# Attention inside a two-model transformer program: one more step of lag between scores and output, four calls joined into one, and a bias added on VectorE

## The reference

```
for one head and one block of 128 queries:
    s = q @ k.T * 64**-0.5  (+ bias, + mask)          # 128 x nk scores
    p = softmax(s)  (with a sink logit in two of them) # rows over nk keys
    o = p @ v
diff_attention:  pd = softmax(s0) - lam * softmax(s1);  o = pd @ v      # two maps, one output
```

## Time and profile before

| | |
|---|---|
| median of three runs | 4613.79 us (4609.85 to 4614.44) |
| the profiled execution | 4609.33 us |
| its span | 4607.6 us |
| TensorE matmul busy | 92% of the span |
| VectorE busy | 67% |
| ScalarE busy | 39% |

### The profile page before, as it was taken

The page is one execution under the profiler, slowest core; times in us unless marked ns, Lnnn a source line. Parts: engine busy times, 40 slices in busy tenths (PEclk is TensorE's granted clock), DMA queues, the critical chain, the costliest instruction groups (busy, mean ns, idle before and its releaser), DMA issues. The chain is left out here.

```text
span 4607.6 us, 87690 instructions
## 1 busy us (share of the span) xinstructions
PE 4230.1 (92%) x33441; PEld 3999.2 (87%) x33450; DVE 3069.0 (67%) x5233; ACT 1815.8 (39%) x2655; POOL 37.9 (1%) x54
## 2 busy tenths in 40 slices
PE   8978999979798489999999899999997889999998
PEld 8956999769784389899999898999997589899998
DVE  5576565555513448887777588877772559887886
ACT  4324343343323334444333444443332344444333
POOL 0000000000000001000000010000000001000000
PEclk9988999989899699999999999999998999999999
DMA  6643666436420046655777475567762047556775
GB/s 231 201 135 110 225 203 226 142 101 226 143 73 19 0 126 209 192 174 176 228 228 228 151 229 177 175 190 228 227 188 75 33 153 229 172 176 193 228 228 180
DMA packets 300376, 786.61 MB, mean 171 GB/s; under 512 B 32849, under 2 KB 132177, under 8 KB 299345
## 3 DMA queue, kind: packets, MB, share of 16 engines
q1 hardware_dynamic: 300112, 782.95, 54.6%
HBM read 731.44 MB, written 51.38 MB: 170 GB/s over the span
## 5 line engine op out<-in xcount | busy, mean ns | idle before, releaser
L264 PE MATMUL banks<-h_parts,ring_hi 128*128 128x256 f32 x7920 | 1981.2, 288 | 114.4 <-ACT ring_hi L247 104.7
L247 ACT ACTIVATE ring_hi<-ring 128x1024 fp32r<-128x1024 f32 x1166 | 1234.4, 1059 | 1962.3 <-PE banks L268 1932.9
L265 PE MATMUL banks<-h_parts,ring_hi 128*128 128x256 f32 x7920 | 1957.8, 284 | 0.0
L253 DVE TENSOR_TENSOR ring_lo<-ring,ring_hi 128x1024 fp32r<-128x1024 f32 x1166 | 1428.4, 1226 | 724.6 <-ACT ring_hi L247 710.6
L264 PEld LDWEIGHTS banks<-h_parts,ring_hi 128*128 128x128 f32 x7920 | 1530.3, 193 | 129.4 <-issue 67.8
L265 PEld LDWEIGHTS banks<-h_parts,ring_hi 128*128 128x128 f32 x7920 | 1531.8, 193 | 0.3
L268 PE MATMUL banks<-h_parts,ring_lo 128*128 128x256 f32 x7920 | 1116.2, 284 | 0.9 <-DVE ring_lo L253 0.6
L268 PEld LDWEIGHTS banks<-h_parts,ring_lo 128*128 128x128 f32 x7920 | 1026.3, 193 | 2.5 <-DVE ring_lo L253 2.5
L1603 DVE TENSOR_TENSOR scratch<-con,picks 128x1024 f32<-128x1024 f32 x192 | 235.2, 1225 | 128.1 <-PE banks L1487 128.1
L264 PE MATMUL banks<-h_parts_ctx,ring_hi 128*128 128x256 f32 x992 | 245.1, 285 | 0.0
L265 PE MATMUL banks<-h_parts_ctx,ring_hi 128*128 128x256 f32 x992 | 243.1, 283 | 0.0
(11 more groups left out here) (207 smaller groups left out, 3248.6 us busy)
## 6 DMA issues: line engine op xcount, KB each, us to landing
ring<-peer_u_dram SPq DMA_DIRECT2D x384, 512.0 KB, 4.0
ring<-peer_v_dram SPq DMA_DIRECT2D x384, 512.0 KB, 3.8
act_store<-acts_out SPq DMA_DIRECT2D x384, 128.0 KB, 3.2
scratch<-act_store SPq DMA_DIRECT2D x384, 128.0 KB, 3.5
ring<-ffn_gate_dram SPq DMA_DIRECT2D x88, 512.0 KB, 3.7
ring<-ffn_up_dram SPq DMA_DIRECT2D x88, 512.0 KB, 3.6
ring<-ffn_down_dram SPq DMA_DIRECT2D x88, 512.0 KB, 3.6
big<-mod_w_dram SPq DMA_DIRECT2D x80, 512.0 KB, 4.5
```

The source lines that it names most:

```text
L247: self.nc.scalar.activation(self.hi[:, n % 2], self.ring[:, self.slot(j)], ACT.Copy).then_inc(self.count("tile_hi").sem, 1)
L253: self.nc.vector.tensor_tensor(self.lo[:, self.slot(j)], self.ring[:, self.slot(j)], self.hi[:, n % 2].bitcast(F32), ALU.subtract).then_in ...
L264: self.nc.tensor.matmul(out, w, b_hi, start=opens and m == 0, stop=False)
L265: self.nc.tensor.matmul(out, w, b_lo, start=False, stop=False)
```

## The change

```diff
+@dataclass
+class Pair:                       # one pair's q, key, v, out, nk, diff, hard, soft, bias, sink, group, block
+def pairs_of(groups, shared, q, keys, v, out, nk, diff=False, hard=False, soft=None, bias=None, sink=None):
+    return [Pair(q[:, j, t * P:(t + 1) * P], keys[:, j // shared, 0:nk], ..., j, t)
+            for j in range(groups) for t in range(T // P)]
-def attention(k, groups, shared, q, keys, v, out, scratch, nk, mask=None, soft=False, bias=None, sinks=None, diff=False):
+def attention(k, pairs, scratch, mask=None):
...
-    st = k.region(o, 2, 16).rearrange("p s (f a) -> p s f a", a=2)
+    st = k.region(o, 4, 16).rearrange("p s (f a) -> p s f a", a=2)
...
-    steps = range(n + 2)
+    steps = range(n + 3)
...
             def scores(p):
...
-                        if bias is not None:
-                            pe.wait_ge(staged[j % 2].sem, staged[j % 2].after(16 * (j // 2 + 1)))
-                            nc.tensor.matmul(near, eight, bs[:, j % 2, a, t], start=False, stop=False)
...
             for i in steps:
                 if i < n:
                     scores(i)
-                if 0 <= i - 1 < n:
-                    turn(i - 1)
                 if 0 <= i - 2 < n:
-                    mix(i - 2)
+                    turn(i - 2)
+                if 0 <= i - 3 < n:
+                    mix(i - 3)
...
             def highest(p):
...
                 dve.wait_ge(scored.sem, scored.after(p + 1))
-                nc.vector.reduce_max(s[:, MAX], k.ps[:, 2 * (p % 2):2 * (p % 2) + 2, 0:nk], AX).then_inc(peak.sem, 1)
+                if x.bias is not None:
+                    dve.wait_ge(staged[x.group % 2].sem, staged[x.group % 2].after(16 * (x.group // 2 + 1)))
+                    nc.vector.scalar_tensor_tensor(both[:, :, 0:T], bs[:, x.group % 2, :, x.block], 1.0 / SCALE, both[:, :, 0:T],
+                                                   ALU.mult, ALU.add).then_inc(biased.sem, 1)
+                    dve.wait_ge(biased.sem, biased.after(biases_to[p + 1]))
+                nc.vector.reduce_max(s[:, MAX], both, AX).then_inc(peak.sem, 1)
...
             def invert(p):
...
-                dve.wait_ge(mixed.sem, mixed.after(p - 1))
+                dve.wait_ge(mixed.sem, mixed.after(p - 3))
...
-                nc.vector.tensor_scalar(eight, k.c("ident"), 1.0 / SCALE, None, ALU.mult).then_inc(ready.sem, 1)
             for i in steps:
...
-                    if not diff:
-                        move(i - 1)
                 if 0 <= i - 2 < n:
-                    keep(i - 2)
+                    move(i - 2)
+                if 0 <= i - 3 < n:
+                    keep(i - 3)
...
             def exps(p):
...
-                act.wait_ge(turned.sem, turned.after(maps * (p - 1)))
+                act.wait_ge(turned.sem, turned.after(earlier(turns_to, p - 1)))
...
             for i in steps:
                 if i < n:
                     exps(i)
-                if 0 <= i - 1 < n:
-                    move(i - 1)
                 if 0 <= i - 2 < n:
-                    keep_spread(i - 2)
+                    move(i - 2)
+                if 0 <= i - 3 < n:
+                    keep_spread(i - 3)
...
 def even_mixer(k, a):
...
-    attention(k, 4, 1, proj[:, 0:4, x_], proj[:, 4:8], v_na, cat[:, 0:4, x_], more, 2 * T, mask=mask, bias=a.na_bias)
-    attention(k, 4, 1, proj[:, 0:4, c_], proj[:, 4:8, c_], v_na[:, 2:4], cat[:, 0:4, c_], more, T)
-    attention(k, 4, 1, proj[:, 8:12, x_], proj[:, 12:16], v_diff, cat[:, 4:8, x_], more, 2 * T, diff=True)
-    attention(k, 4, 1, proj[:, 8:12, c_], proj[:, 12:16, c_], v_diff[:, 2:4], cat[:, 4:8, c_], more, T, diff=True)
+    attention(k, pairs_of(4, 1, proj[:, 0:4, x_], proj[:, 4:8], v_na, cat[:, 0:4, x_], 2 * T, hard=True, bias=a.na_bias)
+              + pairs_of(4, 1, proj[:, 0:4, c_], proj[:, 4:8, c_], v_na[:, 2:4], cat[:, 0:4, c_], T)
+              + pairs_of(4, 1, proj[:, 8:12, x_], proj[:, 12:16], v_diff, cat[:, 4:8, x_], 2 * T, diff=True)
+              + pairs_of(4, 1, proj[:, 8:12, c_], proj[:, 12:16, c_], v_diff[:, 2:4], cat[:, 4:8, c_], T, diff=True), more, mask)
```

More of the change, by code:

```diff
@@ L9 @@
 from contextlib import ExitStack
+from dataclasses import dataclass
 import numpy as np
@@ new lines @@
+@dataclass
+class Pair:
+    q: object
+    key: object
+    v: object
+    out: object
+    nk: int
+    diff: bool
+    hard: bool
+    soft: object = None
+    bias: object = None
+    sink: object = None
+    group: int = 0
+    block: int = 0
+def pairs_of(groups, shared, q, keys, v, out, nk, diff=False, hard=False, soft=None, bias=None, sink=None):
+    return [Pair(q[:, j, t * P:(t + 1) * P], keys[:, j // shared, 0:nk], v[:, :, j // shared * P:(j // shared + 1) * P],
+                 out[:, j, t * P:(t + 1) * P], nk, diff, hard, soft, bias, sink, j, t)
+            for j in range(groups) for t in range(T // P)]
@@ new lines, in attention @@
+def attention(k, pairs, scratch, mask=None):
+    nc, NT, n = k.nc, T // P, len(pairs)
+    staged = [k.dma(f"group_staged_{s}") for s in range(2)]
+    ready, scored, biased, peak, shift, exped, sink_ready, sunk, total, recip, mixable, turned, moved, moved_too, spread, \
+        spread_kept, mixed, kept = map(k.count, (
+            "masks_ready", "scores_done", "bias_added", "row_max", "shift_ready", "exp_done", "sink_shifted", "sink_exp",
+            "row_total", "inverse_total", "maps_combined", "probs_turned", "probs_moved", "probs_moved_too",
+            "inverse_spread", "spread_kept", "mixed_done", "output_kept"))
+    W, o = max(x.nk for x in pairs), scratch
+    pr = k.region(o, 4, W).rearrange("p (s a) t -> p s a t", s=2)
+    pt = k.region(o + 4 * W, 4, W).rearrange("p (s a) t -> p s a t", s=2)
+    o += 8 * W
+    st = k.region(o, 4, 16).rearrange("p s (f a) -> p s f a", a=2)
+    hard = k.region(o + 64, NT, T // 2).rearrange("p t n -> p (t n)").bitcast(BF16).rearrange("p (t n) -> p t n", t=NT)
+    eye = k.region(o + 64 + T, 1, P // 2)[:, 0].bitcast(BF16)
+    factors = k.region(o + 128 + T, 2, P)
+    bs = k.region(o + 384 + T, 2, 4 * T).rearrange("p s (a t n) -> p s a t n", a=2, t=NT)
+    MAX, SHIFT, SUM, SINK_SHIFT, SINK, TOTAL, INVERSE, MIX = range(8)
+    maps = [1 if x.diff else 2 for x in pairs]
+    turns_to = [sum(maps[:p]) for p in range(n + 1)]
+    seconds_to = [sum(m - 1 for m in maps[:p]) for p in range(n + 1)]
+    sinks_to = [sum(x.sink is not None for x in pairs[:p]) for p in range(n + 1)]
+    totals_to = [sum(x.sink is not None or x.diff for x in pairs[:p]) for p in range(n + 1)]
+    biases_to = [sum(x.bias is not None for x in pairs[:p]) for p in range(n + 1)]
+    diffs_to = [sum(x.diff for x in pairs[:p]) for p in range(n + 1)]
+    groups = biases_to[n] // NT
@@ L1075, in _ @@
         def _(sp):
-            if bias is not None:
-                for j in range(groups):
-                    sp.wait_ge(scored.sem, scored.after(NT * (j - 1)))
-                    sp.dma_start(bs[:, j % 2].rearrange("p a t n -> p (a t n)"), bias[j]).then_inc(staged[j % 2].sem, 16)
+            for p, x in enumerate(pairs):
+                if x.bias is not None and x.block == 0:
+                    sp.wait_ge(biased.sem, biased.after(NT * (x.group - 1)))
+                    sp.dma_start(bs[:, x.group % 2].rearrange("p a t n -> p (a t n)"),
+                                 x.bias[x.group]).then_inc(staged[x.group % 2].sem, 16)
         @block.tensor
@@ L1087, in scores @@
                     rows = slice(a * HD, (a + 1) * HD)
[L1088 to L1091, removed]
+                    last = nc.tensor.matmul(bank(p, a), x.q[rows], x.key[rows], start=True, stop=not x.hard and x.soft is None)
+                if x.hard or x.soft is not None:
+                    pe.wait_ge(ready.sem, ready.after(2))
                     for a in range(2):
[L1093 to L1098 removed]
+                        last = nc.tensor.matmul(bank(p, a)[:, 0:T], eye if x.hard else k.c("ident"),
+                                                hard[:, x.block] if x.hard else x.soft[:, x.block], start=False, stop=True)
                 last.then_inc(scored.sem, 1)
             def turn(p):
[L1102 to L1105, removed]
+                x = pairs[p]
+                for a in range(maps[p]):
+                    if x.diff:
+                        pe.wait_ge(mixable.sem, mixable.after(diffs_to[p + 1]))
                     else:
                         pe.wait_ge(exped.sem, exped.after(2 * p + a + 1))
[L1108 to L1109 removed]
+                    pe.wait_ge((moved, moved_too)[a].sem, (moved.after(p), moved_too.after(seconds_to[p]))[a])
+                    for b in range(x.nk // P):
                         last = nc.tensor.transpose(k.ps[:, 4 + a, b * P:(b + 1) * P], pr[:, p % 2, a, b * P:(b + 1) * P],
@@ L1124, in mix @@
                 pe.wait_ge(moved.sem, moved.after(p + 1))
-                if not diff:
[L1126 to L1132, removed]
```

(23 more changed lines are left out.)

104 lines of the change are left out of this document (44 added, 60 removed).

## The result

Six runs of each kernel: 4614.11 us before (4609.85 to 4617.45), **4569.18 us after** (4564.65 to 4573.89), ratio 0.9903 with a 95% interval of 0.989 to 0.9916. That is 44.9 us, where 42.4 were forecast, and 2 us under the predicted 4571. The profiled execution after took 4573.89 us (span 4571.8), the longest of its six.

The account below looks back on a forecast made before the run. A VectorE-ScalarE ring, TensorE's own work, or the differential combination wait bounds each call. Even mixer -43.6 and other calls +1.2 give -42.4: 4566.9 us profiled, 4571 as median; range 4560 to 4589.

Parts of the forecast that it names:

- What bounds each call: Attention calls: VectorE-ScalarE loop in odd mixer (3.95 us), TensorE in even's first call (4.46) and dilated, combination wait in differential (2.65).
- The ring: Odd mixer: closed loop of row maximum, shift, exponentials, ScalarE's copy, spread copy, VectorE's output, next row maximum; 3.95 us a step.
- The lag in differential pairs: Differential calls: the longer lag removes the 2.65 us wait for the combination; pitch from 6.2 to 3.87 us.
- The clock: Differential steps of the joined run: granted clock 1.00, with TensorE busy 2.8 of 3.87 us; before, 0.72 and 0.67.
- the first rival: Differential pairs: clock stays at 1.2 GHz, up to 1.7 us a step over the ring, +17, time 4588; chance 0.12.
- the 2: Last eight steps of the joined run: 2 us added because TensorE may fall to 1.2 GHz for part of them.
- The bias: First eight even pairs: VectorE's addition takes 0.78 us, ring becomes 4.65, minus 0.2 us a step; a gain at the start.
- The first pairs: Start of the joined run: pair 0 at 1425.1, pair 1 +2.2, pair 2 +5.1, pair 3 +8.0, pair 4 +12.9 us.
- Borders and drain: Even mixer: three borders, 27.5 us in all, each replaced by one step; final drain 8 us, before 8.9.
- the prediction's fifth rival: Differential calls: the lag does not remove the wait, only borders are won, some 20 us, time 4594; chance 0.03.
- The other calls: Odd mixer +0.7 (2.4 lost at end, 1.7 won at beginning), windowed +0.2, dilated +0.3; together +1.2, bounds -2 and +5.
- Rival 2: All calls: older pairs' copies free VectorE earlier, the ring loosens and calls go to TensorE's pace, time 4549; chance 0.05.

Follow-up runs that it names:

- the filler: Six bf16 matmuls before TensorE's wait for the combination in each differential pair, against the joined changed kernel with the old lag: 4590.17 us, ratio 0.9955.

## Why the prediction was right

- *What bounds each call.* Right, and it is what the number rests on. The ring was read from one step of the odd mixer, and its copy predicted 3.87 in the differential pairs (3.87 measured), 2.67 with 256 keys (2.69) and 3.95 unchanged in the odd mixer (3.95). Two experiments show that it is the ring and not something beside it: cut at the spread copy, with the same work on every engine, it releases some 20 us; cut at the output, another loop through the output's bank takes its place.
- *The lag in differential pairs.* Right: their window fell from 55.8 us (with its fill and drain) to 30.5 for the same eight pairs, and taking the lag back costs 34.9. The prediction said that the wait makes the slow clock and left open what each costs; the filler, in one profile, shows the first (1.00 once the wait is filled) and gives about half to each.
- *The clock.* I took 1.00 for the differential pairs and added 2 us for the last eight; it was 1.00 in both, so the first rival did not come and the 2 were not needed. (TensorE was also busier there than the 1.5 us a step of the text: 12.2 of 17.0 us in 1521 to 1538, 1.9 in each 2.69.) The rule of the Trainium skill ("TensorE: Matmul & The Clock Gate", "Part 4: PE-mode transpose"), by which transposes don't count toward the faster clock as other matmuls do, cost nothing here: the clock stood at 1.00 with TensorE busy 21.1 of 30.5 us, about a quarter of it transposes. Whether these counted, or the rest was enough without them, no run shows.
- *The bias.* Right in sign and size: 4.65 forecast, 4.60 measured, because the addition took 0.69 and not 0.75 us, the lower bound of the text. Putting it back is within the noise.
- *The first pairs.* A miss of 2.1 us: pair 4 was expected at +12.9 and came at +15.0. The step that failed is pair 2 and 3, where I let TensorE's scores take 1.06 us. They took 2.08: the clock stayed at 1.2 GHz until about 1442.9, 13.4 us after the start (before it rose after 9.6).
- *Borders and drain.* The drain took 6.2 us for the 8 allowed, and with the needless 2 that more than repays the fill. That part of the agreement is luck: the joined run came out at -45.1 for -43.6 because late first pairs (+2.1) and a slower last stretch (+0.5) met a short drain (-1.8) and an allowance that wasn't used (-2). The steady pitches, which carry most of it, were not luck. Joining measured 12.0 us; for the borders alone the prediction's fifth rival had put some 20, too much.
- *The other calls.* +2.8 for +1.2, in the bounds: the odd mixer lost 1.5 (0.7 forecast), windowed 0.9 (0.2), dilated 0.4 (0.3). In the odd mixer the end cost 2.3 as forecast (2.4; last row maximum to last output 10.0 for 7.75), and the beginning won 0.8 where 1.7 stood in the sum: that is the term that was off. Its sign was right: a longer lag costs a call that it doesn't speed up.
- Rival 2 (the ring loosens by itself) did not come; it needed an edit. Taken one by one, the three parts give back 34.9, 12.0 and 2.7 us, 49.6 against 44.9 measured together; each of these medians is known to a few us only, so that says nothing of whether the parts help or hinder each other.

## What to carry to other kernels

When engines with written-out orders wait for each other, walk the timeline from one row maximum (or any event that comes once a step) to the next through "released by" and "stood behind"; the sum of that walk is the pitch, and an edit that doesn't shorten it, a longer lag or work moved to another engine, gave nothing a step here and cost something at the ends. Before an instruction is moved out of such a ring, list every buffer with a single copy that it frees: the next loop may run through it. And an idle gap on TensorE can cost twice, once by itself and once by the clock (1.6 and 1.6 us a pair in the filler's profile).

## What the runs showed of the hardware

- TensorE stayed at 1.2 GHz for the first 13.4 us of the joined run, in which it was busy 11.4 us: 5.2 without a break, a gap of 2.0, and then nearly all of the rest. The first two rows hold that time, the third is what follows:

```profile
1429.50:1436.00 6.50, 5.17 (x12) 1.29 (x12) 3.47 (x7) 2.10 (x4) 0.00 (x0) 0.50 0.46 161
1436.00:1443.50 7.50, 6.66 (x20) 2.98 (x20) 4.18 (x9) 4.01 (x11) 0.00 (x0) 0.54 0.21 73
1443.50:1446.00 2.50, 2.39 (x30) 2.08 (x32) 2.43 (x5) 0.44 (x1) 0.00 (x0) 1.00 0.33 74
```

- It held 2.4 GHz in steps with 2.8 us of work and a gap of 1.06 us in 3.87. In steps with a gap of 2.65 it fell for part of each (0.76), and in the old lag's steps of 5.0 us with a gap of 1.85 it stood at 1.2 GHz throughout (0.50).
- Six bf16 matmuls with zeros for weights, put into those gaps, brought it to 1.00 in both, 1501 to 1524 and 1532 to 1550 (one profile).
- A VectorE multiply-add of 128 by 512 with one source and the output in PSUM took 0.69 us, and the same with all in SBUF 0.75.
